# Scores of attention one pair ahead in banks of their own, both token streams in one sequence, and the first third of the modulation loaded by column halves

## The chip, the cores and the metric

The kernel runs on one core of a Trainium2 chip. The metric is device microseconds of the whole launch, lower is better. Inputs and weights are float32 and lie in HBM; TensorE does the matrix products, ScalarE (ACT) and VectorE (DVE) the rest, GpSimd (POOL) and SyncE (SP) issue the DMAs.

## The reference, cut to what matters

Two layers over 256 latent tokens (stream 1, `x`) and 256 context tokens (stream 0, `ctx`), width 1024. Every vector of scale, shift and gate comes from one product with `w_ada` (1024 x 6144 a layer) and a bias:

```python
for l in range(DEPTH):
    mod = (jax.nn.silu(c) @ w_ada[l] + b_ada[l])[:, None, :]
    mod_c = (jax.nn.silu(c_ctx) @ w_ada[l] + b_ada[l])[None, None, :]
    sh1, sc1, g1, sh2, sc2, g2 = jnp.split(mod, 6, axis=-1)
    h = x * (1.0 + sc1) + sh1
    hc = cx * (1.0 + sc1c) + sh1c
    lat = project_heads(h, w_in[l], ...)      # q, k, v of branches A, B, C and gate logits
    cts = project_heads(hc, w_in[l], ...)
    y = mix_latent(lat, cts, ...)             # three attentions, gated sum, output projection
    x = layer_norm(ALPHA * x + g1 * y, ...)
    h = x * (1.0 + sc2) + sh2
    y = expert_choice_ffn(h, ...)             # router, top 32 tokens of 16 experts, SwiGLU
    x = layer_norm(ALPHA * x + g2 * y, ...)
```

The context goes the same way, except in the last layer, where only its keys and values are wanted. Attention has 6 A heads (window and sink), 4 B heads (low-rank queries and keys) and 6 C heads. Context queries see the 256 context keys, latent queries all 512.

## The kernel before, in words

Each engine has its own program, written out in order; they meet in semaphores. All weights go through a ring of 9 slots of 1 MB; SyncE issues the loads in the order in which TensorE's program asks for them, each as soon as the slot's last reader is done. PSUM has 8 banks: six are handed out in rotation (`begin`, `turn[0] % 6`), bank 7 collects the modulation products, bank 6 turned rows of them. `begin` waits until the bank's last content has been taken (`bank_drained`).

The start. TensorE takes the first third of layer 0's modulation (shift 1 and scale 1, columns 0 to 2048 of `w_ada[0]`) in 8 pieces of 128 rows, one product of four column groups each (`ada_products`). ScalarE copies the sums (`ada_move`), TensorE turns them (`ada_turn`), VectorE adds the bias (`ada_columns`). Only then can the turned tokens be modulated into `hT` (ScalarE the k-tiles 0 to 3, VectorE 4 to 7) and the projections run. `qkv` works off a list of steps: ("P", chunk, t) is the projection of token tile t by one chunk of `w_in`, 8 k-tiles long, chunk 1 first, then 3; "H" turns and modulates a tile; "N", "U", "TB", "TA", "TC" norm, raise and turn heads. In layer 0 a hook (`ada_hook`) behind each "P" and behind steps of attention does one of the 40 remaining modulation products (16 in `qkv`, then one every 9/4 steps), and now and then a move, a turn or rows.

Attention (`attention(l, s, step)`) runs for one stream after the other: 32 units each (a unit is one head with one tile of 128 queries) in len + 5 steps. At step i TensorE does the scores of units i and i+1 (on even i), the hook, the transposes of the probabilities of unit i-3, and, once four units are complete, the product with V for two heads. VectorE takes the maximum of unit i and scales the probabilities of unit i-1; ScalarE does the exponential of unit i, copies the transposes of unit i-3 and the product with V. Probabilities have four buffers: the exponential of unit u waits for the transposes of unit u-4. The last turn of C rows, ("TC", 3), stands inside attention at step 2. At units 24 and 28 of the latent stream ScalarE casts one 1 MB piece of the gate weights (`high`, L1315). Layer 1 has only the latent stream. Then come gates, output projection, routing and the expert stage, which are written as before.

The lines: L519 is the helper `mm` (all products), L564 `transposes`, L539 the turn of modulation rows, L1150 the copy of modulation sums, L1173 and L1456 the modulation of tokens, L1280 the exponential, L1294 and L1300 ScalarE's copies of transposes and of the product with V, L1621 to L1640 VectorE's part, L1030 and L1037 SyncE's loads of `w_ada` and of other weights.

Of the kernel before, what the change touches and what calls it, by code (L numbers as in the profile page):

```python
# [18 lines left out]
P = 128  # L19
# [11 lines left out]
ADA_BANK, TURN_BANK = 7, 6  # L31
GATE_COL = 1696
# [43 lines left out]
H_EARLY = [("H", 0), ("H", 1)]  # L76
FIRST_STEPS = [("P", 1, 0), ("H", 2), ("P", 1, 1), ("H", 3)] + QKV_STEPS[2:]
# [10 lines left out]
def trunk(nc, x, c, ctx_in, c_ctx, w_ada, b_ada, w_in, a_sink, b_q_norm, b_kv_norm, b_w_uq, b_w_ukv, c_q_norm,  # L88
          c_k_norm, w_branch, w_out, ln1_g, ln1_b, w_router, w_gate, w_up, w_down, ln2_g, ln2_b, consts, out):
    es = ExitStack()  # L90
    with es:
# [262 lines left out]
        def units(l, s):  # L354

            return [(4 * j + 2 * q + h, j, h, q) for j in range(8) for q in (0, 1) for h in (0, 1)]

        def unit_base(l, s):
            return 32 * (2 * l + s) if l == 0 else 64
# [23 lines left out]
        def _(pe):  # L383
# [149 lines left out]

            def ada_turn(l, third):

                drained(pe, ("ada", l, third))
                b = begin(("adaT", l, third), bank=TURN_BANK)
                for j in range(4):
                    ins = nc.tensor.transpose(psum[:, b, P * j:P * j + P], modrow[:, P * j:P * j + P], ident)  # L539
                end(ins, b)  # L540

            def ada_rows(l):
                pe.wait_ge(mod_cols, 3 * l + 3)
# [16 lines left out]
            def transposes(key, sources, rows=P, takers=1):  # L560

                b = begin(key, takers)
# [4 lines left out]
            def x_transposes(name, l, t):  # L567
                for j in (0, 1):
                    transposes((name, l, t, j), [X[:, t, k * P:(k + 1) * P] for k in range(4 * j, 4 * j + 4)])

            def qkv(l, steps):
                held, turns = None, 0
                for step in steps:
                    kind, t = step[0], step[-1]
                    cut = l == DEPTH - 1 and t < 2
                    if kind == "H":
                        if l == 0:
                            pe.wait_ge(x_in, 16)
                        else:

                            pe.wait_ge(x_ready, 2 * first_tile(l - 1) + len(tiles(l - 1)) + t + 1)
                        x_transposes("hT", l, t)
                    if kind == "P":
# [5 lines left out]
                        b = begin(("P", l, ch, t), takers=2 if ch != 0 else 1)  # L589
# [5 lines left out]
                        for k in range(KT):  # L595
# [3 lines left out]
                            w, o = held[k // 4][1][:, k % 4, lo:], psum[:, b, lo:width]  # L599
# [37 lines left out]
            def attention(l, s, step):  # L637
                nk = 2 if s == 0 else 4
                us = units(l, s)
                for i in range(len(us) + 5):  # L640
                    if s == streams(l)[0] and i == LAST_TURN_AT:
                        qkv(l, LAST_TURN)
                    for u, j, h, q in us[i:i + 2] if i % 2 == 0 else ():
                        br, first = PAIRS[j]
                        t = 2 * s + q
                        b = begin(("S", l, s, u))
                        if br == "B":
                            mm_in = qT["B"][0:QK_B, first + h, t * P:(t + 1) * P], kT["B"][0:QK_B, first + h, 0:nk * P]
                        else:
                            rows = slice(HD * h, HD * h + HD)  # L650
                            mm_in = qT[br][rows, first, t * P:(t + 1) * P], kT[br][rows, 0:nk * P]
                        if u % 4 == 0 and (j == 0 or PAIRS[j - 1][0] != br):

                            for tt in range(4):
                                drained(pe, (f"T{br}k" if br == "B" else f"T{br}r", l, tt))
                                if br == "B" and not (l == DEPTH - 1 and tt < 2):
                                    drained(pe, ("TBq", l, tt))
                        masked = br == "A" and s == 1
                        ins = mm(psum[:, b, 0:nk * P], *mm_in, True, not masked)
                        if not masked:  # L660
                            end(ins, b)
# [1236 lines left out]
```

## Time and profile before

| | us |
|---|---|
| median of 3 runs (lowest, highest) | 1780.26 (1777.73, 1781.99) |
| profiled execution | 1778.49 |
| its span, first to last instruction | 1776.5 |
| TensorE busy | 1508.5 (85% of the span) |
| VectorE, ScalarE busy | 505.8, 399.7 |
| HBM read | 520.04 MB, 293 GB/s over the span |

Times in the rows count from the span's start. A busy TensorE is not one at its peak: its instructions overlap, and their ends are modelled. "PEclk" is the granted TensorE clock as a share of full speed. An arrow names what ended an engine's idle time.

### The profile page before, as it was taken

To read this page: it belongs to the slowest core of one execution; us is meant where nothing else is said; L and a number is where in the kernel's file an instruction comes from. 1 tells how busy PE (TensorE), PEld (TensorE's weight loads), DVE (VectorE), ACT (ScalarE), POOL (GpSimd) and SP (SyncE) were. 2 spreads that over 40 slices of the span, in tenths; PEclk is the share of its full clock that TensorE was granted. 3 is DMA by queue.
4 is the path that set the end of the run, shared out by engine and by line. 5 is a ranking of instruction groups with operands and counts; after the bars stand their busy time and mean duration, and the time that the engine had idled before them with its cause. 6 is when DMAs were issued, how large, how long until landed. Compare 5 with 4: busy or idle time off the path is not lost.

```text
span 1776.5 us, 22923 instructions
## 1 busy us (share of the span) xinstructions
PE 1508.5 (85%) x9684; PEld 812.0 (46%) x9684; DVE 505.8 (28%) x999; ACT 399.7 (22%) x855; POOL 23.3 (1%) x47
## 2 busy tenths in 40 slices
PE   6999998999978998999888698989977767676764
PEld 2543446888864342433222364568752333232322
DVE  0225576333552000111010534765630000000003
ACT  1213676222232010200000132864320001000000
POOL 1000000000000000000000100000000000000000
PEclk9999999999989999999999899999977777876766
DMA  9645922333467999999999811046889999999995
GB/s 385 215 181 243 386 78 70 103 101 98 182 248 286 421 421 421 422 421 421 421 421 422 308 42 48 1 125 190 355 328 421 421 421 421 421 421 421 420 421 219
DMA packets 98308, 522.67 MB, mean 294 GB/s; under 512 B 10896, under 2 KB 13216, under 8 KB 42912
## 3 DMA queue, kind: packets, MB, share of 16 engines
q1 hardware_dynamic: 94512, 509.97, 71.8%
q0 software_dynamic: 3392, 10.85, 1.8%
q8 instruction: 77, 1.26, 0.3%
q10 hardware_dynamic: 304, 0.40, 0.1%
q14 instruction: 23, 0.19, 0.0%
HBM read 520.04 MB, written 1.15 MB: 293 GB/s over the span
## 4 chain that ended last, share of the span: by engine, by line
PE 54%; SPq 21%; DMA 14%; DVE 7%; ACT 2%; issue 1%; DVEq 0%; ACTq 0%
PE psum L519 50%; SPq L1030 21%; DMA ring<-in_w_down 7%; DMA ring<-in_w_up 4%; PE psum L564 4%; DMA A<-in_w_down 2%; DMA ring<-in_w_ada 1%; ACT hT L1173 1%; DVE X L1651 1%; DVE X L1652 1%; DVE X L1758 1%; DVE small L1621 1%; DVE PR L1640 1%; DVE stats L1764 0%; DVE small L1626 0%
## 5 line engine op out<-in xcount | busy, mean ns | idle before, releaser
L519 PE MATMUL psum<-ring,A 128*32 128x256 f32 (+1 forms) x1920 | 284.3, 562 | 71.1 <-DMA ring<-in_w_up 35.9
L519 PE MATMUL psum<-ring_r,h_hi 128*128 128x512 f32 x704 | 218.4, 392 | 6.9 <-DVE h_lo L1658 5.8
L519 PE MATMUL psum<-A 128*32 128x256 f32 (+5 forms) x1152 | 184.3, 535 | 37.5 <-DMA A<-in_w_up 18.9
L519 PEld LDWEIGHTS psum<-ring,A 128*32 128x32 f32 (+1 forms) x1920 | 90.0, 140 | 250.3 <-issue 108.4
L1792 DVE TENSOR_TENSOR W<-W,psum 128x512 f32<-128x512 f32 (+1 forms) x32 | 17.7, 554 | 547.0 <-PE psum L519 547.0
L519 PE MATMUL psum<-ring,PR 128*32 128x256 f32 (+1 forms) x1080 | 145.8, 504 | 31.4 <-DMA ring<-in_w_down 31.2
L519 PE MATMUL psum<-ring,hT 128*128 128x512 f32 (+3 forms) x512 | 165.9, 479 | 7.5 <-ACT hT L1173 7.3
L519 PE MATMUL psum<-ring_r,h_lo 128*128 128x512 f32 x384 | 150.2, 391 | 0.0
L519 PEld LDWEIGHTS psum<-ring_r,h_hi 128*128 128x128 f32 x704 | 132.5, 189 | 35.3 <-issue 6.6
L519 PEld LDWEIGHTS psum<-ring,hT 128*128 128x128 f32 x512 | 87.2, 196 | 74.2 <-issue 70.3
L519 PEld LDWEIGHTS psum<-A 128*32 128x32 f32 (+3 forms) x1152 | 60.9, 142 | 124.6 <-issue 54.6
L1400 ACT ACTIVATE W<-psum 128x512 f32<-128x512 f32 (+1 forms) x32 | 15.7, 491 | 436.8 <-PE psum L519 436.8
L1658 DVE TENSOR_TENSOR ring_r<-ring,ring_r 128x2048 fp32r<-128x2048 f32 (+2 forms) x44 | 91.6, 2096 | 57.9 <-ACT ring_r L1315 57.7
L519 PEld LDWEIGHTS psum<-ring,PR 128*32 128x32 f32 (+1 forms) x1080 | 49.0, 128 | 122.4 <-issue 68.0
L1315 ACT CAST ring_r<-ring 128x2048 fp32r<-128x2048 f32 (+2 forms) x44 | 77.0, 1754 | 103.5 <-PE psum L519 87.3
L1408 ACT COPY PR<-psum 128x512 f32<-128x512 f32 (+1 forms) x32 | 15.3, 479 | 317.6 <-PE psum L564 317.6
L1805 DVE TENSOR_TENSOR B<-psum,PR 128x512 f32<-128x512 f32 (+1 forms) x32 | 17.9, 558 | 232.6 <-PE psum L519 232.6
L519 PEld LDWEIGHTS psum<-ring_r,h_lo 128*128 128x128 f32 x384 | 72.4, 188 | 15.2
L519 PE MATMUL psum<-ring,cs 128*32 128x512 f32 x384 | 54.6, 642 | 9.4 <-DMA ring<-in_w_ada 7.2
L1280 ACT ACTIVATE PR<-psum,small 128x512 f32<-128x512 f32 (+1 forms) x96 | 58.9, 614 | 11.0 <-issue 6.0
L519 PE MATMUL psum<-ring_r,o_hi 128*128 128x512 f32 x192 | 59.1, 389 | 0.0
L564 PE MATMUL psum<-cst,PR 128*128 128x128 f32 x320 | 51.4, 287 | 9.0 <-ACT PR L1280 7.1
(196 smaller groups left out, 1401.9 us busy)
## 6 DMA issues: line engine op xcount, KB each, us to landing
ring<-in_w_down SPq DMA_DIRECT2D x93, 1024.0 KB, 26.1
ring<-in_w_up SPq DMA_DIRECT2D x85, 1024.0 KB, 25.3
ring<-in_w_gate SPq DMA_DIRECT2D x80, 1024.0 KB, 25.3
ring<-in_w_ada SPq DMA_DIRECT2D x48, 1024.0 KB, 10.9
A<-in_w_up SPq DMA_DIRECT2D x40, 1024.0 KB, 26.0
A<-in_w_gate SPq DMA_DIRECT2D x38, 1024.0 KB, 26.4
ring<-in_w_in SPq DMA_DIRECT2D x36, 1024.0 KB, 5.1
A<-in_w_down SPq DMA_DIRECT2D x28, 1024.0 KB, 26.2
```

What stands on the lines that cost most here:

```text
L519: return nc.tensor.matmul(o, a, b, start=start, stop=stop, skip_group_check=True)
L564: ins = nc.tensor.transpose(psum[0:rows, b, i * P:(i + 1) * P], s, ident)
L1030: sp.dma_start(dst, src).then_inc(landed, 16)
L1173: ins = nc.scalar.activation(hT[:, k, t * P:(t + 1) * P], psum[:, b, i * P:(i + 1) * P], ACT.Identity, scale=modcol[:, l, s, 8 * scale + k ...
L1280: nc.scalar.activation(prob[:, u % 4, 0:nk * P], psum[:, b, 0:nk * P], ACT.Exp, bias=small[:, c4:c4 + 1], accum_out=small[:, c4 + 2:c4 + 3 ...
L1315: nc.scalar.copy(hi, src).then_inc(split_high, 1)
L1621: run(V_.tensor_reduce(small[:, c4 + 3:c4 + 4], psum[:, b, 0:nk * P], AX, ALU.max, negate=True))
L1640: V_.tensor_scalar(prob[:, u % 4, 0:nk * P], prob[:, u % 4, 0:nk * P], small[:, c4 + 2:c4 + 3], None, ALU.mult).then_inc(prob_ready, 1)
L1651: run(V_.scalar_tensor_tensor(xt, xt, small[:, 41:42], norm_g, ALU.subtract, ALU.mult))
L1652: run(V_.scalar_tensor_tensor(X[:, t, :], xt, small[:, 46:47], norm_b, ALU.mult, ALU.add))
L1658: V_.tensor_tensor(lo, src, hi_read, ALU.subtract).then_inc(split_low, 1)
L1805: V_.tensor_tensor(ysb[:, (e - 1) % 8, 0:Wd], psum[:, b, 0:Wd], gate_y[:, 0:Wd], ALU.mult) \
```

## The change

Three parts.

1. The first third of layer 0's modulation comes in two column halves. A piece now has 256 rows and, of both shift and scale, 512 columns (two DMAs of 2 KB rows); four pieces give the modulation of k-tiles 0 to 3. Then the first half of `w_in` chunk 1 is loaded, and with it TensorE does k-tiles 0 to 3 of the first projection for all four token tiles (`first_half`), in banks 0 to 3, while the second four pieces come in; `qkv` adds k-tiles 4 to 7. ScalarE modulates k-tiles 0 to 3 of all tiles, VectorE 4 to 7. The load of the x tokens waits for the fourth piece in place of the eighth.
2. `attention(l, step)` goes over the units of both streams as one sequence (64 in layer 0, 32 in layer 1). Scores go one pair further ahead, into banks 0 to 3 by unit; the transposes have banks 4 and 5, the product with V bank 6.
3. In a step TensorE does transposes, scores, product with V and then the hook; before it was scores, hook, transposes, product with V.

```diff
+SCORE_BANKS, TURNED_BANKS = (0, 1, 2, 3), (4, 5)
+            def first_products(q, kk):
+                if kk == 0:
+                    begin(("ada", 0, "first", q), bank=ADA_BANK)
+                cols = slice(FIRST_WIDTH * q, FIRST_WIDTH * q + FIRST_WIDTH)
+                src = w_ada[0, 256 * kk:256 * kk + 256, 0:2 * D].rearrange("(j p) (c n) -> p j c n", j=2, c=2)
+                n, w = piece(tuple(((slice(0, P), slice(0, 2), c), src[:, :, c, cols]) for c in (0, 1)), 2, 2,
+                             FIRST_WIDTH)
+                for j in (0, 1):
+                    k = 2 * kk + j
+                    for g in range(4):
+                        ins = mm(psum[32 * g:32 * g + 32, ADA_BANK, 0:256], cs[:, k, :],
+                                 w[:, j, g // 2, 256 * (g % 2):256 * (g % 2) + 256], k == 0, k == KT - 1)
...
+            def first_half(t, w):
+                b = begin(("P", 0, 1, t), takers=2, bank=t)
+                drained(pe, ("hT", 0, t, 0))
+                for k in range(KT // 2):
+                    ins = mm(psum[:, b, :], hT[:, k, t * P:(t + 1) * P], w[:, k, :], k == 0, False)
+                return ins
...
-            for k in range(KT):
-                if k == 4:
-                    pe.wait_ge(context_in, 16)
-                    for _, t in H_EARLY:
-                        x_transposes("hT", 0, t)
-                ada_products(0, 0, k)
...
-            ada_turn(0, 0)
+            for kk in range(4):
+                first_products(0, kk)
+            first_turn(0)
+            pe.wait_ge(context_in, 16)
+            for t in (0, 1):
+                x_transposes("hT", 0, t, (0, ), bank=FIRST_BANKS[t])
+            a, w = CHUNKS[1][0]
+            n, first_in = piece([w_in[0, 0:512, a:a + w]], 4, w)
+            for t in (0, 1):
+                first_half(t, first_in)
+            pe.wait_ge(x_in, 16)
+            for t in (2, 3):
+                x_transposes("hT", 0, t, (0, ), bank=FIRST_BANKS[t - 2])
+            for kk in (0, 1):
+                first_products(1, kk)
+            first_half(2, first_in)
+            for kk in (2, 3):
+                first_products(1, kk)
+            for t in (0, 1):
+                x_transposes("hT", 0, t, (1, ), bank=FIRST_BANKS[t])
+            first_turn(1)
+            free(n, first_half(3, first_in))
+            for t in (2, 3):
+                x_transposes("hT", 0, t, (1, ), bank=FIRST_BANKS[t - 2])
...
-            pool.wait_ge(slot_filled[7], 16)
+            pool.wait_ge(slot_filled[3], 32)
             pool.dma_start(X[:, 2:4, :], x.rearrange("b (t p) d -> p (b t) d", p=P)).then_inc(x_in, 16)
...
+            def attention(l, step):
+                us = all_units(l)
+                turn[0] += (TURNED_BANKS[0] - turn[0]) % 6
+                scores(l, us[0:2])
                 for i in range(len(us) + 5):
-                    if s == streams(l)[0] and i == LAST_TURN_AT:
+                    if i == LAST_TURN_AT:
                         qkv(l, LAST_TURN)
-                    for u, j, h, q in us[i:i + 2] if i % 2 == 0 else ():
-                        b = begin(("S", l, s, u))
...
-                    if l == 0:
-                        ada_hook(step)
-                    step += 1
                     if 3 <= i < len(us) + 3:
-                        transposes(("T", l, s, u), [prob[:, u % 4, k * P:(k + 1) * P] for k in range(nk)])
+                        transposes(("T", l, s, u), [prob[:, u % 4, k * P:(k + 1) * P] for k in range(4 if s else 2)],
+                                   bank=TURNED_BANKS[u % 2])
+                    if i % 2 == 0:
+                        scores(l, us[i + 2:i + 4])
...
+                    if l == 0:
+                        ada_hook(step)
+                    step += 1
```

`scores(l, pair)` is the old loop over two units, with `bank=SCORE_BANKS[u % 4]`. The programs of ScalarE and VectorE in attention keep their order within a step and run over the same joined sequence.

TensorE's program at the start. Before, `ring,cs` are the modulation products, `cst,X` the turning of tokens, `cst,modrow` the turn of the modulation, `ring,hT` the first projection:

```order
L997 MATMUL psum<-cst,A 128x16
L519 MATMUL psum<-ring,cs 32x512 x16
L564 MATMUL psum<-cst,X 128x128 x16
L519 MATMUL psum<-ring,cs 32x512 x16
L1006 MATMUL psum<-cst,A 128x96
L539 MATMUL psum<-cst,modrow 128x128 x4
L519 MATMUL psum<-ring,hT 128x512 x8
L519 MATMUL psum<-ring,cs 32x512 x4
L564 MATMUL psum<-cst,X 128x128 x8
L519 MATMUL psum<-ring,hT 128x512 x8
```

The same place in the changed kernel:

```order
L530 MATMUL psum<-ring,cs 32x256 x32
L568 MATMUL psum<-cst,modrow 128x128 x2
L610 MATMUL psum<-cst,X 128x128 x8
L530 MATMUL psum<-ring,hT 128x512 x8
L610 MATMUL psum<-cst,X 128x128 x8
L530 MATMUL psum<-ring,cs 32x256 x16
L530 MATMUL psum<-ring,hT 128x512 x4
L530 MATMUL psum<-ring,cs 32x256 x16
L610 MATMUL psum<-cst,X 128x128 x8
L568 MATMUL psum<-cst,modrow 128x128 x2
L530 MATMUL psum<-ring,hT 128x512 x4
L610 MATMUL psum<-cst,X 128x128 x8
```

Half of the modulation products, and their turn, have moved behind the first half projections; each `ring,hT` group is 4 k-tiles where it was 8.

TensorE's program in the C heads of layer 1, in the kernel before. `A 128x512` is a pair of scores, `cst,PR` the transposes (four a unit), `W,A` the product with V:

```order
L564 MATMUL psum<-cst,PR 128x128 x4
L519 MATMUL psum<-A 128x512 x2
L564 MATMUL psum<-cst,PR 128x128 x8
L519 MATMUL psum<-A 128x512 x2
L564 MATMUL psum<-cst,PR 128x128 x4
L519 MATMUL psum<-W,A 64x256 x8
```

The same heads in the changed kernel:

```order
L610 MATMUL psum<-cst,PR 128x128 x8
L530 MATMUL psum<-A 128x512 x2
L610 MATMUL psum<-cst,PR 128x128 x8
L530 MATMUL psum<-A 128x512 x2
L530 MATMUL psum<-W,A 64x256 x8
```

The scores of a pair now stand directly ahead of the product with V, and one pair earlier against the transposes.

## Rows read from the trace of the kernel before

**Rows 1.** Busy time of each engine, clock, DMA share and GB/s by stretch.

```profile
600.00:700.00 100.00, 95.07 (x574) 37.86 (x572) 4.83 (x7) 12.51 (x27) 0.00 (x0) 1.00 1.01 421
...
1300.00:1776.00 476.00, 323.68 (x3716) 145.72 (x3716) 45.04 (x93) 30.44 (x69) 0.00 (x0) 0.75 0.95 394
```

**Rows 2.** Timeline of the start: start us, us, engine, line, operation [idle before].

```profile
16.65 1.91 PE L519 MATMUL psum<-ring,cs 128*32 128x512 f32 x8 [0.40 <-DMA ring<-in_w_ada]
...
26.59 1.07 PE L519 MATMUL psum<-ring,cs 128*32 128x512 f32 x8 [1.42 <-DMA ring<-in_w_ada]
...
27.73 0.59 ACT L1150 COPY modrow<-psum 128x512 f32<-128x512 f32 x1 [21.08 <-PE psum L519]
...
28.41 0.89 PE L539 MATMUL psum<-cst,modrow 128*128 128x128 f32 x4 [0.52 <-ACT modrow L1150]
...
31.52 9.08 PE L519 MATMUL psum<-ring,hT 128*128 128x512 f32 x16 [2.22 <-ACT hT L1173]
...
40.52 1.07 PE L519 MATMUL psum<-ring,cs 128*32 128x512 f32 x8
...
42.45 7.03 PE L519 MATMUL psum<-ring,hT 128*128 128x512 f32 x16
...
44.34 0.34 DVE L1523 SCALAR_TENSOR_TENSOR B<-psum,small,PR 128x128 f32<-128x128 f32 x1
...
68.35 2.34 PE L519 MATMUL psum<-ring,hT 128*128 128x160 f32 x16
```

**Rows 3.** DMA issues: KB each, median us from issue to landing.

```profile
X<-in_ctx POOLq DMA_DIRECT2D x1, 1024.0 KB, 12.8
```

**Rows 4.** DMA view of 10 to 12.5, 15 to 17.5, 27.5 to 30 us.

```profile
q1 hardware_dynamic: 90, 0.74, 70.5%
q0 software_dynamic: 84, 0.34, 34.0%
...
DMA packets 145, 1.06 MB, mean 423 GB/s; under 512 B 16, under 2 KB 16, under 8 KB 16
...
DMA packets 487, 0.96 MB, mean 386 GB/s; under 512 B 16, under 2 KB 16, under 8 KB 487
```

**Rows 5.** Busy times in attention of layer 0 and of layer 1.

```profile
162.00:283.10 121.10, 111.77 (x754) 53.51 (x754) 82.49 (x263) 84.24 (x247) 2.74 (x5) 1.00 0.58 227
1099.60:1168.00 68.40, 57.10 (x337) 32.29 (x336) 51.88 (x133) 50.17 (x124) 2.12 (x4) 0.93 0.07 23
```

**Rows 6.** Waits of TensorE from 1100 to 1210 us: total, times, longest.

```profile
PE psum L564 <- DVEq L1427: 4.1, 1, 4.1
PE psum L564 <- ACT PR L1280: 3.2, 3, 1.4
...
PE psum L519 <- ACT PR L1280: 1.9, 3, 0.9
```

**Rows 7.** Timeline of attention in layer 1, with both casts of ScalarE.

```profile
1109.25 0.68 DVE L1621 TENSOR_REDUCE small<-psum 128x1 f32<-128x512 f32 x1
...
1110.88 0.68 DVE L1621 TENSOR_REDUCE small<-psum 128x1 f32<-128x512 f32 x1
...
1150.05 1.90 ACT L1315 CAST ring_r<-ring 128x2048 fp32r<-128x2048 f32 x1
1150.26 1.13 PE L519 MATMUL psum<-A 64*128 64x512 f32 x4
...
1152.52 0.59 ACT L1294 COPY W<-psum 128x512 f32<-128x512 f32 x1
...
1152.78 1.06 PE L564 MATMUL psum<-cst,PR 128*128 128x128 f32 x8 [1.39 <-ACT PR L1280]
...
1157.68 1.90 ACT L1315 CAST ring_r<-ring 128x2048 fp32r<-128x2048 f32 x1
...
1166.04 1.95 PE L519 MATMUL psum<-W,A 128*64 128x256 f32 x16 [0.93 <-ACT W L1294]
```

**Rows 8.** Waits of TensorE from 150 to 290 us, attention of layer 0.

```profile
PE psum L564 <- ACT PR L1280: 3.9, 4, 1.4
```

More of the change, by code:

```diff
@@ L558, in ada_hook, with transposes @@
                     ada_products(*due["products"])
-            def transposes(key, sources, rows=P, takers=1):
-                b = begin(key, takers)
+            def transposes(key, sources, rows=P, takers=1, bank=None):
+                b = begin(key, takers, bank)
                 for i, s in enumerate(sources):
@@ L594, in qkv @@
                             drained(pe, ("hT", l, t, 1))
-                        for k in range(KT):
+                        k_first = KT // 2 if second_half else 0
+                        for k in range(k_first, KT):
                             if t == 0 and k % 4 == 0:
@@ L635, in qkv, with scores @@
                         transposes((kind + "r", l, t), q + [knat[:, t % 2, :]])
-            def attention(l, s, step):
-                nk = 2 if s == 0 else 4
-                us = units(l, s)
+            def scores(l, pair):
+                for s, u, j, h, q in pair:
+                    br, first = PAIRS[j]
+                    t, nk = 2 * s + q, 4 if s else 2
+                    b = begin(("S", l, s, u), bank=SCORE_BANKS[u % 4])
+                    if br == "B":
+                        mm_in = qT["B"][0:QK_B, first + h, t * P:(t + 1) * P], kT["B"][0:QK_B, first + h, 0:nk * P]
+                    else:
+                        rows = slice(HD * h, HD * h + HD)
+                        mm_in = qT[br][rows, first, t * P:(t + 1) * P], kT[br][rows, 0:nk * P]
+                    if u % 4 == 0 and (j == 0 or PAIRS[j - 1][0] != br):
+                        for tt in range(4):
+                            drained(pe, (f"T{br}k" if br == "B" else f"T{br}r", l, tt))
+                            if br == "B" and not (l == DEPTH - 1 and tt < 2):
+                                drained(pe, ("TBq", l, tt))
+                    masked = br == "A" and s == 1
+                    ins = mm(psum[:, b, 0:nk * P], *mm_in, True, not masked)
+                    if not masked:
+                        end(ins, b)
+                for s, u, j, h, q in pair:
+                    if PAIRS[j][0] == "A" and s == 1:
+                        pe.wait_ge(masks_ready, 1)
+                        b = groups["S", l, s, u][0]
+                        at = 256 + P * (1 - q)
+                        end(mm(psum[:, b, at:at + P], ident16[:, :], mask16[:, q, :], False, True), b)
@@ L1821, in _ @@
                     ada_hook(QKV_TURNS - 1)
-                for s in streams(l):
-                    step = attention(l, s, step)
+                step = attention(l, step)
                 n_gates = 6 * first_tile(l)
```

186 lines of the change are left out of this document (101 added, 85 removed).

## The prediction, made before the changed kernel was run

> **What bounds the kernel now.** I read the busy times by stage first [rows 1]. From 600 to 700 us the DMA queues move 421 GB/s at a share of 1.01, and from 1300 us to the end they are at 0.95: the two expert stages run at the pace of their weights. Their loads are released by the gate stage, which stands behind attention and behind the start, so a microsecond taken out of the start or of attention moves the expert stage by a microsecond. None of the changed code lies in the expert stages. The other stages are in-order work of TensorE. The timeline of the start comes second [rows 2]: TensorE waits piece by piece for `w_ada`, the eighth product starts at 26.59, the first projection only at 31.52, and from there it is dense up to 68.35, where the second chunk of `w_in` begins. Third is attention: TensorE is busy 111.77 of 121.10 us in layer 0 and 57.10 of 68.40 in layer 1 [rows 5]. So 9.3 and 11.3 us are all that attention can give while its work stays the same.
>
> **The start.** Removed: the wait of all projection work for all 8 MB of the first third. Nothing is computed less; half of the first projection chunk (four groups of 4 k-tiles) is done while the second half of the modulation loads. Step by step:
>
> 1. When the first half's last piece is there. In the kernel before, the fourth product starts at 16.65 [rows 2]; with the first bytes at about 3 us that is 13.65 us of transfer at the rate of 8 KB rows, 1.06 MB in 2.5 us. The new pieces have 2 KB rows, and a window of those moved 0.96 MB, 386 GB/s against 423 [rows 4]. 13.65 x 423/386 = 15.0, so about 17.9.
> 2. The product then lasts 1.91 (fourth product) or 1.07 (eighth) [rows 2]: TensorE is at its lower or its upper clock level, 1.2 or 2.4 GHz. It stays 16,384 columns in all, now 256 wide.
> 3. From the end of the last product (27.66) to the first projection (31.52) there were 3.86 us. Half of the row copy (0.59) and half of the turn (0.89) go, 0.7 together [rows 2]: 3.2. The first half projection starts at 22.1 (upper level) to 23.0 (lower).
> 4. From 31.52 to 68.35 are 36.8 us of dense work. Now this stretch also holds the four products of the second half, one turn and 8 more X transposes. Between 40.52 and 42.45 lie one product and 8 X transposes, so about 1.0 for each: 4.0 + 0.3 + 1.0 = 5.3. Sum 42.1. In it is the loss of the first projection to the clock: 9.08 against 7.03 of the next, 2.05 [rows 2]. If the engine is at its upper level when it starts, 40.1.
> 5. So the second chunk starts at 22.1 + 40.1 = 62.2 or 23.0 + 42.1 = 65.1, against 68.35: 6.2 or 3.3 earlier. I take 4.7: TensorE works densely from about 18 on with gaps near one microsecond, which speaks for the upper level, but the fourth product before was still at the lower.
>
> What can be late instead. The x tokens: their load now starts behind the fourth piece, at about 18, and TensorE waits for them after two half projections, at 22.1 + 6.9 = 29.0 to 23.0 + 8.9 = 31.9 (7.03/2 each, 2.05 more at the lower level). A load of the same size and queue, the context's, took 12.8 us from issue to landing [rows 3]: that would give 31, a wait of up to 2. But it ran beside 8 KB rows. From 10 to 12.5 us its queue moved 84 packets, 0.34 MB, beside 90 packets, 0.74 MB, of the other [rows 4]: the two queues alternate packet by packet. Against 2 KB packets 4 KB ones get two thirds of about 0.96 MB per 2.5 us, and 1.05 MB take about 4 us in place of 7.7; 12.8 - 3.7 = 9 us, so x is there at 27 and I take no wait. The page "DMA: Bandwidth & Descriptors" of the Trainium skill, section on queues, rings and completion order, has the engines alternate between queues at packet granularity too, but with 9 to 17 descriptors to a packet, and its fit of 2.0 us plus bytes/436e3 would make it 4.4 us for the whole load; by that x would be there at 22.4, and the sum is the same. The second half's last piece comes after 6.3 MB more, 16.3 us at 386 GB/s, at about 34; TensorE wants it at 36 to 38, so that is hidden. After the first half group of P(1,0) ends, the normalised rows came 3.9 us later (first projection done at 40.6, last of them at 44.34 + 0.34, [rows 2]: 4.1); a hook product and the next half group, 1.0 + 3.4, just cover it. The mask tables and the small parameter loads start some 10 us later and are wanted after 70.
>
> **Attention.** Removed: between the two streams of layer 0 one drain and refill of five steps. Moved: each pair of scores goes one pair ahead of its use; the hook moves to the end of the step. Added: the scores of unit i+3 now stand before the transposes of unit i-2 in TensorE's order, and wait for the bank that the exponential of unit i-1 has to leave; and the transposes have two banks of their own, so those of unit u wait for ScalarE's copy of unit u-2. All further TensorE work queues behind either wait.
>
> Layer 1, place by place. At the beginning TensorE waits 4.1 for the last C rows from VectorE [rows 6]; the scores of units 2 and 3 now fill part of it. That is worth nothing by itself: VectorE's maxima start where they did and then come every 1.63 us (1109.25, 1110.88 [rows 7]). Walking the steps with these durations, scores 7, 9 and 11 wait for the exponentials of 3, 5 and 7 (0.6 to 1.0 each). When the second pair's product with V is done I find the new order 1.2 us ahead, in place of the 2.1 that its waits up to there came to: 1.9 in three on the exponentials, of which the last, 0.25, comes later, and 0.4 of the 3.2 whose rest are the casts [rows 6]. The 0.25 goes too: 1.4 ahead.
>
> In the C heads ScalarE twice puts a cast of 1.9 us between two units (1150.05 and 1157.68), and TensorE waited 1.4 each time [rows 7]. After, counted from the end of the product with V, 0.4 before the cast: the cast ends at 2.2, the exponential of unit 25 at 2.9 (TensorE's wait ended 0.8 after the cast's end), the copies of 22 and 23 at 3.4 and 4.5 (0.59 a copy). TensorE does transposes 22 and 23 and one score (1.6 us, two scores being 1.13), then score 29 waits for exponential 25 until 2.9, and transposes 24 and 25 wait for copies 22 and 23. This product with V to the next comes to 8.1 us where it was 7.6 (the casts' distance), and from the second to the end 10.7 as before, since there ScalarE's order sets the pace. The pair of scores ahead (1.06) was already paid in front of it. Together 1.6 lost. Net for layer 1: 0.2 slower.
>
> Layer 0, the same reading. The beginning: scores 4 and 5 now wait for exponentials 0 and 1, but VectorE's pace with 256 columns hides it, and I find TensorE 0.6 ahead after the first pair. Of the 3.9 us of waits for ScalarE [rows 8] 2.8 are the casts; 1.1 in the middle, and 0.4 of small ones, go with the refill. Hook products move no column more or less. 0.6 + 1.5 - 1.6 = 0.5 gained.
>
> Bounds for attention: no more than 4 gained in layer 0 and 5 in layer 1 (9.3 and 11.3 less the wait for the first exponentials and the last products, that no order hides); no less than 2 lost in each, by the waits just listed, twice as long.
>
> **The sum.** 4.7 + 0.5 - 0.2 = 5.0 us. The profiled execution took 1778.49 (span 1776.5), the median is 1780.26; the difference is taken off the median: 1775.3.
>
> **Rivals.**
> - The waits of attention are filled. For it: more scores stand ready at any time, and 20.6 us of idle are there. Against it: VectorE's pace at the beginning and the casts. Worth 4 + 5 in place of 0.3: 1780.3 - 4.7 - 9 = 1766.6. Chance 0.15.
> - Slower: the scores' wait for an exponential holds back transposes that are ready. It decides where VectorE or ScalarE, not TensorE, sets the pace of a pair; then each pair of the A and C heads of the wide stream waits about 1 us: 10 to 11 pairs a layer, 21 us, of which half lies in idle time that is there anyway. 1780.3 - 4.7 + 10.5 = 1786. For it: VectorE's 1.63 per A unit [rows 7] is close to TensorE's own 57.10/32 = 1.78 [rows 5]. Against it: it is still below, and in layer 0 the hook products give TensorE more still. Chance 0.11.
> - The start gives back what it wins: lower clock level throughout, and x late by the old 12.8 us: 3.3 less up to 2. With attention unchanged 1779. Chance 0.16.
> - My forecast, 1775.3, its own range 1772.5 to 1778: 0.58.
>
> What the measurement can tell from no change is about 0.2%, 3.6 us. The forecast lies beyond it in about three quarters of its cases; with the first rival 0.59 faster, with the rest of the forecast and most of the third 0.29 the same, 0.12 slower. The range leaves out the fastest part of the first rival and the slower one: 1768.5 to 1780.5.
>
> **What would show it.** Start: a first projection at 22 to 23 us, no DMA wait for x, the second chunk of `w_in` (128x160) at 62 to 65. If x keeps TensorE waiting, step 5 is wrong. Attention of layer 1: from the first scores to the last product with V 68.4 us as before, with a wait for the exponential behind each cast. If it takes under 64, the walk through the steps is wrong; if waits for the exponential stand at every pair, the slower rival is right. The expert stages should keep their length.

## The result, and the profile after

The changed kernel takes 1786.66 us (median of 11, 1780.37 to 1793.18) against 1778.92 of the kernel before beside it (median of 11, 1776.86 to 1781.99): ratio 1.0045, 95% interval [1.0028, 1.0062]. It is slower where 1775.3 was forecast, and above the range. Its runs lie over 13 us, those of before over 5. The profiled execution took 1784.1 us with a span of 1782.0, 5.5 more than before.

The start first. The timeline of the kernel after (start us, duration us, engine, line, operation, tile names, shapes, idle time before and what ended it):

```profile
17.77 1.94 PE L530 MATMUL psum<-ring,cs 128*32 128x256 f32 x16 [0.78 <-DMA ring<-in_w_ada]
...
23.38 7.11 PE L530 MATMUL psum<-ring,hT 128*128 128x512 f32 x16 [1.31 <-ACT hT L1248]
30.32 1.04 PE L610 MATMUL psum<-cst,X 128*128 128x128 f32 x8
...
64.84 2.44 PE L530 MATMUL psum<-ring,hT 128*128 128x160 f32 x16 [1.22 <-DVEq L1505]
```

Against [rows 2] the first projection stands at 23.38 instead of 31.52, there is no wait for x at 30.32, and the second chunk of `w_in` starts at 64.84 instead of 68.35: 3.5 us won. Then attention. TensorE's timeline through the last heads of layer 0:

```profile
263.24 1.12 PE L530 MATMUL psum<-A 64*128 64x512 f32 x2
265.24 1.12 PE L530 MATMUL psum<-A 64*128 64x512 f32 x2 [0.87 <-ACT PR L1355]
266.29 1.60 PE L610 MATMUL psum<-cst,PR 128*128 128x128 f32 x8
...
269.83 2.29 PE L530 MATMUL psum<-W,A 128*64 128x256 f32 x16
...
275.63 0.63 PE L610 MATMUL psum<-cst,PR 128*128 128x128 f32 x4 [2.50 <-ACT W L1369]
276.79 0.63 PE L610 MATMUL psum<-cst,PR 128*128 128x128 f32 x4 [0.53 <-ACT W L1369]
277.35 3.63 PE L530 MATMUL psum<-W,A 128*64 128x256 f32 x16
...
287.77 1.19 PE L530 MATMUL psum<-ring_r,h_hi 128*128 128x512 f32 x2 [2.89 <-DVE h_lo L1750]
```

The score behind the cast waits (0.87), the transposes of the second cast wait (2.50), both as the walk in the prediction had them. But the product with V (128x256, x16 in its row) takes 3.63 us where it is 1.95 in every such row of before ([rows 7] has one), and the gates' first pair takes 1.19 where before has 0.70. The table by stretches (length, busy us and instructions of PE, PEld, DVE, ACT, POOL, then TensorE's granted clock, DMA share, GB/s) shows the clock; first after, then before:

```profile
260.00:290.00 30.00, 22.27 (x119) 12.63 (x118) 17.18 (x30) 20.51 (x38) 2.11 (x4) 0.85 0.21 63
```

```profile
265.00:275.00 10.00, 7.68 (x48) 3.81 (x46) 5.59 (x13) 9.27 (x17) 0.00 (x0) 1.00 0.00 1
275.00:285.00 10.00, 6.42 (x52) 4.68 (x52) 7.25 (x10) 6.88 (x16) 2.12 (x4) 1.00 0.27 84
```

Before, the clock stays at 1.00 (2.4 GHz) there although TensorE is busy only 77 and 64%; after it drops for part of the time to 1.2 GHz. From the first scores to the end of the last product with V layer 0's attention takes 126.4 us where it took 121.2, layer 1's 73.1 where it took 68.4. The waits of TensorE in it hardly change (9.2 against 9.0 in layer 0, 10.9 against 11.3 in layer 1). It is its busy time that grows, by 5 us a layer, for the same matmuls.

Two things are in that growth. One is the clock. From 262 to 284.9 us of layer 0 it is at 0.85 on average, which is 3.4 us of full speed lost where before loses none; over layer 1's attention it is 0.91 against 0.93, about 1.8 us more lost. The other is in the scores. The two scores of a pair of A or C heads (64*128 in their rows) run side by side: in before such a pair (x4 in its row) takes 1.13 us ([rows 7], at 1150.26), and in the rows above one score alone (x2) takes 1.12. Where the second score has to wait, the pair takes longer, up to twice as long, at the same clock, and the profile counts most of it as busy. Here are all such scores of layer 1's attention (busy us, mean ns of one, idle before them), before and after:

```profile
L519 PE MATMUL psum<-A 64*128 64x512 f32 x48 | 15.4, 724 | 0.0
```

```profile
L530 PE MATMUL psum<-A 64*128 64x512 f32 x48 | 19.0, 731 | 3.7 <-ACT PR L1355 3.7
```

That is 3.6 of the 5.0 us there; either kernel has two of these pairs at the lower clock. In layer 0 these scores take 25.9 us against 22.3, and about 1 us of it is a pair at the lower clock (2.08, at 267.82).

The expert stages keep their pace of 421 GB/s. So: 3.5 won at the start, 5.2 and 4.7 lost in the two attentions. That is 0.9 more than the 5.5 between the two profiles: the stretch between the attentions, whose code is the same, took 814.6 us here and 816.5 in before (816.2 in a second profile of the changed kernel, e12).

### The profile page after: what moved, and what is told of

Read it like the earlier page. It is cut to its first block and busy times, and to the rows that moved or that the text cites. A ratio compares the mean times of both kernels' runs of the same rounds, so it can differ in the third digit from the quotient of the medians.

```text
span 1782.0 us, 23076 instructions
## 1 busy us (share of the span) xinstructions
PE 1513.9 (85%) x9748; PEld 816.7 (46%) x9748; DVE 506.3 (28%) x1002; ACT 397.2 (22%) x856; POOL 23.2 (1%) x47
## 5 line engine op out<-in xcount | busy, mean ns | idle before, releaser
L530 PE MATMUL psum<-ring,A 128*32 128x256 f32 (+1 forms) x1920 | 279.4, 550 | 76.2 <-DMA ring<-in_w_up 40.3
L530 PE MATMUL psum<-A 128*32 128x256 f32 (+5 forms) x1152 | 191.4, 538 | 42.1 <-DMA A<-in_w_up 17.4
L530 PEld LDWEIGHTS psum<-A 128*32 128x32 f32 (+3 forms) x1152 | 65.1, 145 | 133.0 <-issue 55.6
L1897 DVE TENSOR_TENSOR B<-psum,PR 128x512 f32<-128x512 f32 (+1 forms) x32 | 17.9, 558 | 232.8 <-PE psum L530 232.8
L530 PEld LDWEIGHTS psum<-ring_r,h_lo 128*128 128x128 f32 x384 | 72.8, 189 | 15.4
L530 PE MATMUL psum<-ring_r,o_hi 128*128 128x512 f32 x192 | 59.1, 389 | 0.0
L530 PE MATMUL psum<-ring,cs 128*32 128x512 f32 (+1 forms) x448 | 54.2, 577 | 3.5 <-DMA ring<-in_w_ada 3.5
```

Of the source, the lines that this page charges most:

```text
L530: return nc.tensor.matmul(o, a, b, start=start, stop=stop, skip_group_check=True)
L1897: V_.tensor_tensor(ysb[:, (e - 1) % 8, 0:Wd], psum[:, b, 0:Wd], gate_y[:, 0:Wd], ALU.mult) \
```

## The experiments

Each was timed beside the kernel before: e1 to e4 beside a before of 1778.12 us (23 runs), e5 to e8 beside 1777.93 (17), e9 to e12 beside 1778.33 (23). The last two columns are TensorE's time from the first scores to the end of the last product with V, in brackets the waits in it, from one profile each. Line numbers differ by kernel.

| kernel | median us | ratio to before [95%] | layer 0 | layer 1 |
|---|---|---|---|---|
| before | 1778.9 | 1 | 121.2 (9.0) | 68.4 (11.3) |
| changed | 1786.7 | 1.0045 [1.0028, 1.0062] | 126.4 (9.2) | 73.1 (10.9) |
| e12, changed, second time | 1785.6 | 1.0045 [1.0033, 1.0057] | 127.6 (8.6) | 71.2 (10.1) |
| e1, start alone | 1774.1 | 0.9979 [0.9967, 0.9991] | 121.1 (9.0) | 68.4 (11.1) |
| e2, attention alone | 1789.1 | 1.0074 [1.0059, 1.0089] | 127.9 (8.9) | 71.7 (10.3) |
| e3, scores not ahead | 1779.3 | 1.0011 [1.0002, 1.0019] | 123.5 (7.7) | 69.8 (10.8) |
| e4, three dummy products | 1784.1 | 1.0037 [1.0024, 1.0049] | 126.9 (6.6) | 70.1 (7.8) |
| e5, start and joined streams | 1773.8 | 0.9978 [0.9969, 0.9988] | 119.6 (7.8) | 68.4 (11.5) |
| e6, dummy products at all seams | 1782.9 | 1.0026 [1.0015, 1.0036] | 127.2 (6.6) | 72.0 (5.4) |
| e7, third bank in layer 1 | 1784.5 | 1.0035 [1.0022, 1.0047] | 128.6 (9.2) | 70.9 (9.7) |
| e8, ahead, banks in turn | 1828.8 | 1.0284 [1.0269, 1.0298] | 159.1 (27.4) | 84.3 (18.0) |
| e9, e5 with fixed banks | 1777.6 | 1.0001 [0.9993, 1.0010] | 122.7 (7.9) | 69.8 (10.5) |
| e10, changed, hook first | 1781.8 | 1.0017 [1.0005, 1.0028] | 124.4 (8.8) | 71.7 (10.1) |
| e11, changed, casts late | 1783.9 | 1.0036 [1.0024, 1.0049] | 126.9 (8.5) | 70.5 (9.8) |

### The two halves: e1 and e2

```diff
 # e1: the new start, attention as before
-                step = attention(l, step)
+                for s in streams(l):
+                    step = attention(l, s, step)
 # e2: the new attention, the start as before
```

> The changed kernel with the attention of before (stream after stream, scores not ahead, banks in rotation), so the new start alone. Theory A (the start gains, attention loses): in the profiles the second chunk of w_in began 3.5 us earlier than before (64.84 against 68.35); with the attention of before that arrives at the end: 1778.9 - 3.5 = 1775.4. Theory B (the loss comes with the start, whose smaller DMA rows or shifted ring slots hurt later): as slow as the changed kernel, 1784 to 1789.

> The kernel before with the new attention and the old start. Theory A: attention took 126.4 us in place of 121.1 in layer 0, the gates after it began at the lower clock level (1.6 more), and in layer 1 it took 4.7 more: 11.5 in all, so 1778.9 + 11 = 1790. Theory B: 1779 or less, since the waits that remain are of the same sum in the trace (9 us in layer 0 in both).

Both came out as their theory A has it. The start alone wins: 4.0 us between the medians, by the ratio 3.7. The new attention alone costs 11. Their sum, 7 us lost, is close to the changed kernel's 7.7. The term of 4.7 for the start stands; the 0.3 for attention is the one that failed.

### Which part of the attention change costs: e3, e5, e9, e10

```diff
 # e3: the changed kernel, scores issued in their own step (fixed banks, hook last)
-                        scores(l, us[i + 2:i + 4])
+                        scores(l, us[i:i + 2])      # ahead of the transposes
 # e9: e3 with the hook between scores and transposes, as before
+                    if l == 0:
+                        ada_hook(step)
 # e5: e9 with all groups taking the six banks in turn, as before
-    b = begin(("S", l, s, u), bank=SCORE_BANKS[u % 4])
+    b = begin(("S", l, s, u))
 # e10: the changed kernel (scores ahead) with the hook ahead of transposes and scores
```

> The changed kernel with the scores of units i and i+1 issued at step i again, in the new banks (0 to 3 by unit), transposes in banks 4 and 5, both streams in one sequence. Theory A1 (it is the pair ahead that loses: the scores wait for the exponential of unit i-1): score 29 no longer waits behind the cast; 2 us a layer back and with them the fall of the clock: near 1779. Theory A2 (it is the two banks of the transposes): transposes 28 still wait 2.5 us for the copy behind the second cast in each layer, and it stays at 1784 to 1788.

> The new start, and in attention only one thing of the change: both streams as one sequence of units. Scores stand at their own step again, all groups of products take the six banks in turn as before, and layer 0's modulation work stands behind the scores as before. If the joining itself costs nothing and what e3 lost against the start alone (5.2 us: 1779.3 against 1774.1) comes from fixed banks and the place of the modulation work: 1774 us or below, layer 0's attention at or under 121.1 us, TensorE's granted clock 1.00 to the end of it. If the joined seam is what makes the clock fall in layer 0's last heads: near 1779 us, a last but one product with V of 3.6 us there, and gates that start at 1.19 us a pair.

> As e5 (new start, streams joined, scores at their own step, layer 0's modulation work behind the scores and ahead of the transposes) with one thing added: the fixed banks, four for scores, two for transposes, one for products with V. It stands between e5 (1773.8 us, attention of layer 0 in 119.6 us) and e3 (1779.3 us, 123.5 us). If the fixed banks cost, through the two banks of the transposes (the waits of 1.3 us for ScalarE's copies at units 26 and 30 that e3 has): near 1779 us, with those waits and the lower clock behind them. If the place of the modulation work costs: near 1774 us in layer 0, and layer 1, which has no such work, keeps e3's 69.8 us against 68.4.

> The changed kernel with layer 0's modulation work ahead of the transposes and the scores of each step, where it stood behind them. If its new place costs TensorE the cover for the exponentials at the start of layer 0's attention (the wait of 2.3 us there): the wait falls to about 0.5 us, and the whole is 3 us under the changed kernel. If the clock in the heads of branch C of both layers is what counts, nothing changes by over 1.5 us: there is hardly modulation work left there.

These make a ladder. e1 to e5, joining the streams: layer 0's attention gets 1.5 us shorter in the profile, the whole time does not tell them apart (0.9979 and 0.9978); in e5's profile layer 0's gates behind it start at the lower clock (1.09 us for the first pair), which can take the gain back. e5 to e9, the fixed banks: 0.23%, about 4 us, intervals apart. Scores ahead: e9 to e10 0.16%, where the intervals overlap, e3 to the changed kernel 0.34%, apart. Hook last: e9 to e3 0.10%, where they overlap, e10 to e12 0.28%, 5 us, apart. So the fixed banks cost; scores ahead cost clearly only with the hook last, and the hook last only with the scores ahead.

e5 met its first expectation. e3 came out at the 1779 of A1, but the last but one product with V takes 3.60 and 3.22 us there, so the low clock in the last heads does not need the pair ahead. e9 fell between its two; that layer 1, which has no modulation work, takes e3's 69.8 again speaks for the banks.

What the banks do is seen by setting layer 0's waits in e5 and in e9 side by side (engine, tile, line waited at, releaser: total us, times, longest), e5 first:

```profile
PE psum L610 <- ACT PR L1352: 3.0, 3, 1.4
```

```profile
PE psum L610 <- ACT W L1368: 3.1, 3, 1.3
...
PE psum L610 <- ACT A L1331: 1.4, 1, 1.4
```

The wait changed its cause, not its size: in e5 the transposes wait for the exponential that they transpose, in e9 for ScalarE's copies, which empty the two banks (L1368 the copies of transposes; L1331, once, the copy of the last turned C rows). Layer 0's attention waits 7.8 us in all in e5 and 7.9 in e9. But e9's last but one product with V takes 3.29 us, e5's 1.95. TensorE's timeline in e9 behind layer 0's second cast:

```profile
274.01 0.63 PE L610 MATMUL psum<-cst,PR 128*128 128x128 f32 x4 [1.29 <-ACT W L1368]
275.16 0.63 PE L610 MATMUL psum<-cst,PR 128*128 128x128 f32 x4 [0.53 <-ACT W L1368]
275.72 3.29 PE L530 MATMUL psum<-W,A 128*64 128x256 f32 x16
```

And in e5, same place:

```profile
272.21 1.50 PE L610 MATMUL psum<-cst,PR 128*128 128x128 f32 x12 [1.40 <-ACT PR L1352]
273.96 1.95 PE L530 MATMUL psum<-W,A 128*64 128x256 f32 x16 [0.25 <-ACT W L1366]
```

Behind one wait of 1.40 and twelve transposes in a row the product ran at the upper clock; behind 1.29, four transposes, 0.53 and four more it did not. Layer 1 has the same in both kernels (1.95 and 3.25 us).

### The seam into attention: e12, and what e10 shows there

> The changed kernel once more, on the same chip as these, with a second profile. If the lower clock at the start of layer 0's attention, which four of the variants with scores ahead show at 165 to 180 us and the changed kernel's own profile does not, belongs to it too: it may show here, with an attention of 127 to 130 us in layer 0, and times between 1780 and 1793 us again. If it belongs to the variants alone: 126.4 us again.

A second profile of the changed kernel shows what its first had hidden. The first rows are the first profile, the second fence is e12:

```profile
165.82 1.33 PE L530 MATMUL psum<-A 64*128 64x256 f32 x4 [2.33 <-ACT PR L1355]
167.08 1.06 PE L530 MATMUL psum<-ring,cs 128*32 128x512 f32 x8
```

```profile
167.20 1.85 PE L530 MATMUL psum<-A 64*128 64x256 f32 x4 [2.32 <-ACT PR L1355]
168.99 1.93 PE L530 MATMUL psum<-ring,cs 128*32 128x512 f32 x8
```

Same order, same wait of 2.3 us, and behind it the same eight modulation products take 1.06 us or 1.93. The table by stretches of e12 has the clock:

```profile
165.00:170.00 5.00, 2.80 (x12) 1.20 (x12) 3.48 (x18) 4.11 (x13) 0.00 (x0) 0.63 1.02 429
170.00:175.00 5.00, 5.00 (x33) 1.98 (x25) 3.13 (x14) 2.75 (x13) 0.53 (x1) 0.50 1.00 421
175.00:180.00 5.00, 5.00 (x36) 2.23 (x30) 3.42 (x16) 3.08 (x13) 0.00 (x0) 0.85 1.02 421
```

0.50 is 1.2 GHz. This drop stands in the profiles of e2, e4, e6, e7, e11 and e12, all with scores ahead and the hook last; only the changed kernel's first profile escaped it. From the first scores to the start of the sixth last product with V of layer 0 it is 85.4 us in that one and 88.8 to 89.5 in the six: 3.4 to 4.1 us. (In e3 and e9, whose scores are not ahead, waits of 2.0 and 1.4 us for ScalarE stand there, and the clock over 165 to 175 us is 0.83.) Whether it makes the spread of 13 us over the runs is not shown: a profile shows one run only, and the five runs of e12 lie within 4.3 us. In e10 the modulation products stand ahead of the waiting score (filling half of it), the wait is 1.33, and the clock stays at 1.00:

```profile
163.54 1.06 PE L530 MATMUL psum<-ring,cs 128*32 128x512 f32 x8
165.94 1.33 PE L530 MATMUL psum<-A 64*128 64x256 f32 x4 [1.33 <-ACT PR L1355]
```

Where 3 us were expected from e10, 3.8 came between its median and e12's, 4.9 against the changed kernel's first set; the wait was expected to fall to 0.5 and fell to 1.33.

### Is it the clock or the waits: e4 and e6

```diff
 # e4: ahead of the scores and transposes behind the casts
+                            keep_busy(1)   # between scores 28 and 29 of the wide stream
+                            keep_busy(2)   # ahead of its transposes 28
 # keep_busy(n): n products into a bank whose content nobody reads
+                    mm(psum[:, ADA_BANK, :], ident, hT[:, 0, :])
 # e6: e4, and at i == 3 of each attention fill(4, 2 or 3), ahead of layer 1's last
 # turned tiles fill(4, 3), and ahead of the first gate products twelve of 128x128
```

> The changed kernel with idle TensorE time filled: one product of 128x512 whose result nobody reads between scores 28 and 29 of the latent stream, and two before its transposes 28, in both layers. They lie in waits of 0.87 and 2.5 us. Theory C (a part of the loss is TensorE's clock, which fell to its lower level in the middle of the C heads in both layers, after these waits: the product with V took 3.63 in place of 1.95, the first gates 1.19 in place of 0.70 a pair): the clock stays up, 2 to 4 us a layer come back: 1779 to 1783. Theory not C (the waits alone cost): unchanged, 1786, or 1 to 2 us more by the added work.

> The changed kernel with products into a bank whose content is not used, in each place where TensorE waits for a chain of VectorE and ScalarE: two ahead of the first transposes of exponentials in layer 0's attention, three there and three ahead of the last turned tiles in layer 1's, one and two in the heads of branch C of both layers (as in e4), and twelve small ones (128x128) ahead of the first gate product of each layer. They are meant to lie inside waits. If the clock is what the attention lost: both gates start at 0.70 us a pair, every product with V takes 1.95 us, the attention takes at most 122 us and 69 us, and the whole 1776 us or below. If waits and banks are what it lost and the clock only follows: attentions of 125 and 71 us or more with the clock at its upper level, and 1782 us or more.

With dummy work inside the waits all products with V are back at 1.95 us in both layers of e4, although nothing useful was added: there the clock is the cause of the longer products. Layer 1's attention takes 70.1 us, against 73.1 and 71.2 in the two profiles of the changed kernel. The difference lies behind the fifth product with V, where the casts are: from its end to the end of attention e4 takes 19.3 us, the changed kernel 22.4 and 20.5. So the clock costs 3.1 us there in one profile and 1.1 in the other.

It does not cost all. Before takes 18.3 us for that stretch and 68.4 for the attention, and e4's clock over layer 1's attention is the 0.93 that before has [rows 5]:

```profile
1100.08:1170.15 70.07, 62.15 (x343) 33.86 (x342) 51.36 (x133) 49.39 (x124) 2.12 (x4) 0.93 0.07 22
```

Of its 62.15 us busy about 3.0 are dummy products, so 59.1 are left against 57.1 in before; its scores with 64 rows take 18.1 us where before's take 15.4. 1.6 us of the longer attention remain at the same clock. The pairs of scores that were pulled apart stand in these rows; no run tests them alone.

With the twelve ahead of the gates (two records each in the trace) their first pair takes 0.70 in both layers of e6, here layer 1:

```profile
1173.89 2.94 PE L530 MATMUL psum<-cst 128*128 128x128 f32 x24
1176.86 0.70 PE L530 MATMUL psum<-ring_r,h_hi 128*128 128x512 f32 x2
```

In the whole time, 1784.1 and 1782.9, a gain is not shown: both intervals overlap those of the changed kernel, and e4 missed the 1779 to 1783 of its theory C. In layer 0 neither helped the seam: in e6 I had put the filler at step 3, and the 2.3 us wait stands in step 2, at the scores of units 4 and 5. The filler came behind the wait, as additional work at the lower clock (165 to 170: 0.70, 170 to 175: 0.62). e6's first expectation (attentions of 122 and 69 us, 1776) failed. The figures of its second came (127.2 and 72.0 us, 1782.9), with the clock nearly at its upper level in layer 1 only (0.98), so they too say that the clock is not all; but part of the 72.0 is the dummy work itself, as the first product with V ends 25.0 us after the first scores where it is 23.1 in e4. Dummy products are a probe here, not a cure.

### What makes the waits: e7, e11 and e8

```diff
 # e7
-                                   bank=TURNED_BANKS[u % 2])
+                                   bank=(TURNED_BANKS + (ADA_BANK,))[(i - 3) % 3] if l else TURNED_BANKS[u % 2])
 # e11
-EARLY_SPLITS_AT = (24, 28)
+EARLY_SPLITS_AT = (30, 31)
 # e8: the changed order, bank arguments left out, all groups take six banks in turn
```

> The changed kernel with a third bank for the transposes of exponentials in layer 1, where the bank of the modulation products is free; layer 0 is as in the changed kernel. If two banks for them are the bound: the wait of 2.5 us ahead of unit 28's transposes goes, the last but one product with V is back at 1.95 us, and layer 1's attention falls from 73.1 us to 69.5 us, with 1783 us for the whole. If the wait is one for the exponential itself (late behind the cast), a third bank moves nothing by more than 0.5 us: 73 us and 1786 us.

> The changed kernel with ScalarE's two casts of 1.9 us in the heads of branch C put behind the exponentials of units 30 and 31, where they stood behind those of units 24 and 28. If the casts ahead of the exponentials make the waits of 0.9 and 2.5 us and with them the fall of the clock: both waits go, the last but one product with V takes 1.95 us in both layers, and each layer's attention ends 2 to 4 us earlier; a part comes back as a longer wait ahead of the gates: 1781 us. If the clock falls without them: products with V of over 3 us stay, 1786 us.

> The changed kernel with its order of work, scores a pair ahead and both streams joined, but every group of products takes the six banks in turn as before. If the split of the banks (four for scores, two for transposes, one for products with V) costs: at least 3 us less than the changed kernel, about 1782 us, with attentions of 124 and 70 us. If the order costs and not the banks: within 2 us of the changed kernel, 1786 us.

e7: a third bank turned the wait of 2.5 for a copy into one of 2.21 for the exponential itself. TensorE's timeline in its layer 1:

```profile
1164.81 1.53 PE L610 MATMUL psum<-cst,PR 128*128 128x128 f32 x12
1168.55 0.66 PE L610 MATMUL psum<-cst,PR 128*128 128x128 f32 x4 [2.21 <-DVE PR L1732]
1169.66 3.46 PE L530 MATMUL psum<-W,A 128*64 128x256 f32 x16 [0.46 <-ACT W L1369]
```

So behind a cast the exponential is late either way, and the low clock stays. The attention of 70.9 us lies between the two expectations (69.5 and 73) and is like that of e12 (71.2), which has two banks; a gain from the bank is not shown.

e11: with the casts moved the waits of 0.87 and 2.5 go and the last but one product with V, which had taken 2.6 to 3.6 us, takes 1.95. The drop moved to the last product, behind new waits at the end:

```profile
1167.53 0.71 PE L610 MATMUL psum<-cst,PR 128*128 128x128 f32 x4 [1.66 <-ACT W L1369]
1169.11 3.68 PE L530 MATMUL psum<-W,A 128*64 128x256 f32 x16 [0.88 <-ACT W L1369]
```

Each layer's attention is shorter than in e12 by only 0.7 us, where 2 to 4 were expected, and the intervals of the whole time overlap. So where the casts stand matters little: the waits came back further on, and the low clock with them.

e8 is 42 us slower than the changed kernel where 4 us less or no change were expected: I had the sign wrong. If the bank of a group of transposes is taken from the common turn, it is one that still holds a score issued ahead, and TensorE waits for that score's exponential: in layer 0's attention 25 us of such waits in 26 pieces (3.0 the longest), in layer 1 14.

```profile
PE psum L610 <- ACT PR L1353: 17.4, 16, 3.0
PE psum L530 <- ACT PR L1353: 7.6, 10, 1.7
```

In this kernel scores ahead need banks of their own; without scores ahead, the same fixed banks cost the 4 us seen in e9.

## Why the prediction was wrong

**The start was right, at the weak end.** The fourth product started at 17.77 (said: 17.9), at the lower clock with 1.94 us, the first half projection at 23.38 (22.1 to 23.0; the wait before it was 1.31). x landed 8.9 us after issue (said: 9), without a wait, and while it moved the two queues took packet by packet, with two thirds of the bytes for x, as reckoned (22.5 to 24 us: packets, MB, share):

```profile
q0 software_dynamic: 98, 0.40, 68.2%
q1 hardware_dynamic: 99, 0.20, 35.0%
```

The fit of the Trainium skill, "DMA: Bandwidth & Descriptors", section "Anatomy of one DMA — SWDGE (gpsimd) path", had made it an estimated 4.4; here the measurement decides. The second chunk stood at 64.84, and at 66.44 in e1, whose first half projections took 8.85 us instead of 7.11: over all profiles with the new start 64.8 to 67.8, where 62.2 to 65.1 was said. Short by the wait of 1.22 us for VectorE ahead of it, which a hook product and a half group were to "just cover", and by the clock. In time the start gave 3.7 to 4.0 of the 4.7.

**Attention is the term that failed: 0.3 us gained in the sum, 11 us lost in e2.** The step is the one that adds waits and calls the rest of TensorE's work fixed ("its work stays the same"). The waits kept their sum; TensorE's busy time rose by 5 us a layer. Part of it is the clock, which fell behind the new waits: 3.1 us in layer 1's last heads (1.1 by e12's profile), shown by e4. Part is that pairs of scores no longer run side by side: the walk took about 0.5 us, half a pair, for one score ("one score (1.6 us, two scores being 1.13)", with 1.06 for the transposes), and one alone takes 1.12. The bounds for attention ("no less than 2 lost in each") were drawn from waits alone, so the range could not hold it.

Behind the casts the walk was near the truth as long as the clock stayed up. It said 8.1 us from one product with V to the next and 10.7 from there to the end; before has 7.6 and 10.6, e4 8.3 and 11.1, the changed kernel 9.7 and 12.7 in its first profile, e12 8.3 and 12.2.

**Layer 1's beginning was wrong.** The walk found it 1.4 ahead once the second pair's product with V is done. That product ends 29.8 us after the first scores in before and 30.6 in both profiles of the changed kernel: 0.8 behind. The scores of units 4 and 5 wait for exponential 0, 2.8 us in the first profile and 2.3 in e12, a wait that the walk has only in layer 0; and the next three pairs take 1.30 to 1.63 us (first profile) in place of 1.13.

**Layer 0's beginning was wrong outright.** "scores 4 and 5 now wait for exponentials 0 and 1, but VectorE's pace with 256 columns hides it, and I find TensorE 0.6 ahead after the first pair": this wait is 2.3 us and nothing hides it (the hook work, which had stood there, was moved behind it), and the clock drop at 165 us follows it in six of seven profiles. e10 puts work back there and wins 4 us. That is the hook's place in all steps, not in this one alone.

**The two banks of the transposes** were named as a wait and priced only at the casts. e9 prices all the fixed banks together, four for scores, two for transposes, one for products with V: 4 us, with the sum of waits in layer 0 unchanged. That it is the two, the waits for copies in e9 suggest; e7's third bank in the changed kernel did not show it.

**The slower rival had the time (1786) and not the mechanism.** It wanted a wait of about 1 us for an exponential at each of 10 pairs; layer 0 has two such waits, 3.2 us in all. In a small form it is there: in five more pairs of layer 1 the second score comes 0.2 to 0.5 us late, behind the first and so not counted as a wait. That the time agrees is chance.

**What stays open.** Why the same wait of 2.3 us was followed by the lower clock in six profiles and not in the seventh; and how much the pulled-apart pairs cost in time. e10 against e9, scores ahead with the hook first, says something of it: e10 is 1.6 us longer in layer 0 and 1.9 in layer 1, with waits 0.9 longer and 0.4 shorter. In layer 1 both have a granted clock of 0.90, so it is not the clock there, and e10's scores with 64 rows are busy for 18.4 us where e9's take 15.4. A kernel with scores ahead whose pairs are issued only when both banks are free was not run. A version with the wait of step 2 fully filled was not tried.

**The version to keep** is the new start without the new attention: e1 (1774.1 us) or, with the streams joined and nothing else, e5 (1773.8), 0.2% under the kernel before and 0.7% under the changed one.

## What to carry to other kernels

Where TensorE waits for another engine, an edit that only moves the waits can still cost. Look where the granted clock stands behind each wait: here dense work behind new waits of 1.3 to 2.5 us took up to twice its time. Look also for products that run side by side, and keep both ready at once: counting a pair as two halves is wrong when one half comes alone. Prefetching by issue order on an engine that works in order puts the prefetched instruction's own wait in front of work that is ready; leave filling work (here the modulation products) ahead of it. Split a change along its parts before believing its sum: here one half was worth 4 us and was hidden by the other.

## What the runs showed of the hardware

- More busy time did not mean a higher clock: in before 6.42 of 10 us were busy at a granted clock of 1.00, in the changed kernel 22.27 of 30 at 0.85, in the same place.
- The same program with the same order and the same wait got 1.06 or 1.93 us for the same eight products. A profile of one run can hide a drop that other profiles of the same order have.
- A product with V took 1.95 us wherever the clock was at its upper level, and 2.0 to 3.7 where a part or most of it ran at the lower.
- Two scores of 64 rows each ran in 1.13 us side by side and in 1.12 us each alone, at the same clock.
- Two loading DMA queues took turns by packets: 98 of 4 KB against 99 of 2 KB in 1.5 us, so the one with the larger packets got two thirds of the bytes.
